# Block 2's stick-breaking: suffix sums collected on VectorE, one product with the -1 matrix a step

## The reference

```python
z = jnp.einsum('bqhd,bkhd->bhqk', qb, k).astype(jnp.float32) * scale
strict = kpos[None, :] < qpos[:, None]
log_beta = jax.nn.log_sigmoid(z)
log_rem = jnp.where(strict, jax.nn.log_sigmoid(-z), 0.0)
suffix = lax.cumsum(log_rem, axis=3, reverse=True) - log_rem
a = jnp.where(strict, jnp.exp(log_beta + suffix), 0.0).astype(v.dtype)
return jnp.einsum('bhqk,bkhd->bqhd', a, v)
```

## Time and profile before

| | us |
|---|---|
| median of 3 runs | 3445.26 |
| lowest and highest run | 3442.79, 3449.83 |
| span of the profiled execution (first to last instruction) | 3442.4 |
| TensorE busy | 3355.2 |
| VectorE busy | 1669.0 |
| ScalarE busy | 1222.1 |

### The profile page before, as it was taken

One profiled execution on the slowest core, in us unless ns is written; L12 is line 12 of the kernel. 1 busy time (PEld: TensorE's weight loads), 2 busy tenths in 40 slices (PEclk: granted clock), 3 DMA queues, 4 the chain that ended last, 5 costly groups with the idle time before them and its releaser, 6 DMA issues. The chain is left out here.

```text
span 3442.4 us, 42159 instructions
## 1 busy us (share of the span) xinstructions
PE 3355.2 (97%) x15712; PEld 2626.8 (76%) x15716; DVE 1669.0 (48%) x2158; ACT 1222.1 (36%) x1831; POOL 238.6 (7%) x268
## 2 busy tenths in 40 slices
PE   8999999999999999999999999999999999999998
PEld 6667888775688877888775688887888776678887
DVE  6755443666444344443636554435443544654433
ACT  4343122432522233332444443324233344543233
POOL 1200000011000000000103300002000101300000
PEclk9999999999999999999999999999999989999999
DMA  6213322221243232332220133333332321023332
GB/s 169 63 48 86 97 98 97 86 80 49 73 103 95 98 104 73 97 98 98 75 64 25 38 103 97 97 98 94 96 94 97 86 74 32 20 86 98 97 98 67
DMA packets 434263, 288.19 MB, mean 84 GB/s; under 512 B 44529, under 2 KB 412317, under 8 KB 433897
## 3 DMA queue, kind: packets, MB, share of 16 engines
q1 hardware_dynamic: 431272, 280.02, 28.1%
q0 software_dynamic: 2736, 4.58, 0.9%
q10 hardware_dynamic: 144, 2.10, 0.2%
HBM read 284.53 MB, written 2.13 MB: 83 GB/s over the span
## 5 line engine op out<-in xcount | busy, mean ns | idle before, releaser
L2022 PE MATMUL bank<-hh,whi 128*128 128x512 f32 x2768 | 1093.3, 395 | 16.2 <-DVE hl L1470 7.2
L2023 PE MATMUL bank<-hl,whi 128*128 128x512 f32 x2768 | 1080.1, 390 | 0.0
L2024 PE MATMUL bank<-hh,wlo 128*128 128x512 f32 x2768 | 1079.9, 390 | 0.0
L1404 DVE TENSOR_TENSOR wlo<-raw,whi 128x1024 fp32r<-128x1024 f32 (+2 forms) x534 | 646.4, 1212 | 312.4 <-ACT whi L945 298.0
L945 ACT ACTIVATE whi<-raw 128x1024 fp32r<-128x1024 f32 (+2 forms) x534 | 546.4, 1034 | 258.3 <-PE bank L2024 257.9
L2022 PEld LDWEIGHTS bank<-hh,whi 128*128 128x128 f32 x2768 | 521.4, 188 | 150.3 <-issue 33.0
L2024 PEld LDWEIGHTS bank<-hh,wlo 128*128 128x128 f32 x2768 | 521.1, 188 | 109.4
L2023 PEld LDWEIGHTS bank<-hl,whi 128*128 128x128 f32 x2768 | 521.2, 188 | 108.3 <-issue 2.6
L2022 PE MATMUL bank<-fshi,whi 128*128 128x512 f32 (+1 forms) x1358 | 526.3, 388 | 3.6 <-ACT G L1090 1.6
L2023 PE MATMUL bank<-fslo,whi 128*128 128x512 f32 (+1 forms) x1358 | 522.6, 385 | 0.0
L2024 PE MATMUL bank<-fshi,wlo 128*128 128x512 f32 (+1 forms) x1358 | 522.5, 385 | 0.0
(11 more groups left out here) (257 smaller groups left out, 2565.9 us busy)
## 6 DMA issues: line engine op xcount, KB each, us to landing
raw<-in_ffn_w_gate SPq DMA_DIRECT2D x88, 512.0 KB, 3.8
raw<-in_ffn_w_up SPq DMA_DIRECT2D x88, 512.0 KB, 3.8
raw<-in_ffn_w_down SPq DMA_DIRECT2D x88, 512.0 KB, 3.5
raw<-in_w_in SPq DMA_DIRECT2D x78, 512.0 KB, 3.9
raw<-in_w_up SPq DMA_DIRECT2D x64, 512.0 KB, 4.0
raw<-in_w_down SPq DMA_DIRECT2D x64, 512.0 KB, 3.4
raw<-in_w_out SPq DMA_DIRECT2D x16, 512.0 KB, 4.0
raw<-in_w_in SPq DMA_DIRECT2D x18, 256.0 KB, 3.4
```

The costliest lines, as they stand in the source:

```text
L1404: dve.tensor_tensor(slot3(wlo, s, m), slot3(raw, s, m), slot3(whi, s, m).bitcast(F32), ALU.subtract).then_inc(c.lo_done.sem, 1)
L2022: pe.matmul(o, wh, ah, start=start, stop=False)
L2023: pe.matmul(o, wh, al, start=False, stop=False)
L2024: return pe.matmul(o, wl, ah, start=False, stop=stop)
```

## The change

A new entry ("sb_add", s) is put behind z_dve for the steps with s % 4 = 1 and 2. In it VectorE adds, in place, the tile of the next key block onto the tile of this one (over the queries that both have), when suf(s) has read it. Tile jt + 1 then holds the sum of all later blocks' softplus, and suf(s) takes one product with `minus` and not two or three. suf(s) for s % 4 = 2 and 3 waits for the sum.

```diff
@@ plan_block2
         if s < n_stick:
             stick_steps.append(("z_dve", s))
+        if s and (s - 1) % QT in (1, 2):
+            stick_steps.append(("sb_add", s - 1))
         if s and s % QT == 0:
@@ VectorE
+                    elif s[0] == "sb_add":
+                        p, jt, zb = stick_step(s[1])
+                        dve.wait_ge(c.sb_suf.sem, c.sb_suf.at(l, s[1] + 1))
+                        later = stick_tile(B_SP, jt)[:, :, P:S - P * jt]
+                        dve.tensor_tensor(later, later, stick_tile(B_SP, jt + 1), ALU.add).then_inc(c.sb_add.sem, 1)
@@ TensorE
                         pe.wait_ge(c.sb_sp.sem, c.sb_sp.at(l, s[1] + 1))
+                        if s[1] % QT >= 2:
+                            pe.wait_ge(c.sb_add.sem, c.sb_add.at(l, stick_sums(s[1] - 1)))
                         for head in range(2):
                             ins = pe.matmul(bank[:, zb + head, 0:n], tri, stick_tile(B_SP, jt)[:, head, :], start=False, stop=jt == QT - 1, skip_group_check=True)
-                            for j2 in range(jt + 1, QT):
-                                ins = pe.matmul(bank[:, zb + head, P * (j2 - jt):n], minus, stick_tile(B_SP, j2)[:, head, :], start=False,
-                                                stop=j2 == QT - 1, skip_group_check=True)
+                            if jt < QT - 1:
+                                ins = pe.matmul(bank[:, zb + head, P:n], minus, stick_tile(B_SP, jt + 1)[:, head, :], start=False, stop=True, skip_group_check=True)
                         ins.then_inc(c.sb_suf.sem, 1)
```

More of the change, by code:

```diff
@@ L622, in counts_of @@
             c.sb_suf = signal("sb_suf", 0, n_stick)
+            c.sb_add = signal("sb_add", 0, SB_H)
             c.sb_a = signal("sb_a", 0, n_stick)
@@ L687, in stick_tile, with stick_sums @@
             return g(at + 2 * SB_AT[jt], 2 * n).rearrange("p (e n) -> p e n", e=2)
+        def stick_sums(s):
+            return 2 * (s // QT) + s % QT
         def stick_step(s):
```

## The result

The changed kernel takes 3468.95 us (median of 4 runs, 3467.49 to 3469.83), the kernel before 3444.03 us beside it (4 runs, 3439.09 to 3449.83). The ratio is 1.0075, with a 95% interval of 1.0062 to 1.0087: 25 us slower. A second comparison, of runs of its own, gave 3467.04 and 1.0065 (1.0044 to 1.0086). The forecast was 3456.5, the range 3449.5 to 3464.

What follows compares the result with a forecast made beforehand. TensorE, busy 97% of the span, bounds the kernel. Waits net of removed work 7.0 us, clock 3.4 + 0.8, together 11.2 us slower: 3445.3 + 11.2 = 3456.5 us, range 3449.5 to 3464.

Steps and rivals of the forecast that it cites:

- the moves are worth more than the arithmetic: suf(2) ahead of nq1, suf(6) ahead of gatesf: a layer loses 3.5 us although 3.48 us of work goes.
- The links: Chain waits on TensorE: z(3) 0.6 us, suf(2) 2.25, z(4) 1.05, suf(7) 6.2; both layers lose 7.0 net.
- The removed work: Products dropped from suf(2), suf(3), suf(6), suf(7): 3.48 us less TensorE work a layer, 6.96 in both.
- The clock term: TensorE's clock falls after waits: 2 x 1.7 us behind suf(7), 0.8 us behind suf(2).
- the one loss at z(3) that is in the old time: Low clock behind the second layer's 2.05 us wait ahead of z(3), priced 1.57 us, already in the old time.
- Rival F: The low clock lingers in four places, adding up to 13 us to the 7: +15 to +20, 3463; chance 0.10.
- A: Work counts, order does not; only the sum ahead of suf(7) shows: gain 5.8 us, 3439.5; chance 0.05.
- B: TensorE fills its waits ahead of suf(2) and suf(7) from nq1 and nkw: 3438.3 us; chance 0.02.
- C: Waits partly taken up by idle links behind them, clock mostly holds: +2 to +6.5, some 3450; chance 0.13.
- D: Waits come as worked out, clock holds or falls once: +7 to +9, some 3453; chance 0.17.
- TensorE's busy time: Sign to look for: TensorE's busy time falls by less than 7 us, as the lower clock adds to it.

Runs made afterwards that it cites:

- order_only: The kernel before's arithmetic (all old products, no sums) in the changed kernel's order: 3455.19 us, ratio 1.0032.
- old_order: The changed kernel with every other entry where it stood before, each sum right behind the next step's z_dve: 3447.65 us, ratio 1.0005.
- padded: old_order plus the removed products done again as useless ones: 3445.23 us, ratio 1.0004.
- after_padded: The changed kernel plus the removed products done again into a bank nobody reads: 3469.85 us, ratio 1.0073.
- after_again: The changed kernel itself measured once more, nothing altered: 3467.04 us, ratio 1.0065.
- best_old_sums: The kernel before, all its products in, with suf_exp(1), z_act(7) and z_dve(7) moved up: 3438.18 us, ratio 0.9990.
- best: The change's arithmetic in the old order, with suf_exp(1), z_act(7), z_dve(7) moved up and each sum behind the suf freeing its tile: 3436.48 us, ratio 0.9978.
- filled_last: The changed kernel with 26 useless products in the wait ahead of suf(7) only: 3460.21 us, ratio 1.0045.
- suf6_moved: old_order with suf(6) moved right behind z(7), ahead of gatesf, step 6's sum behind z_dve(7): 3450.97 us, ratio 1.0027.
- filled: The changed kernel with useless products in two waits a layer, 9 ahead of suf(2), 26 ahead of suf(7): 3454.21 us, ratio 1.0031.

## Why the prediction was wrong, point by point

- **That the moves are worth more than the arithmetic: right.** order_only is slow without the sums, old_order is not slow with them. But the sums more than double what the order costs, as they stand in the waits that it opens.
- **The links: right, nearly to the digit.** z(3) waits 0.62 us (0.6 forecast), suf(2) 2.15 (2.25), z(4) 1.00 (1.05), suf(7) 5.83 (6.2). The last is 0.35 us less, as the swap snks itself waited 0.35 for an eviction; the 6.2 counted that as standing still. All thirteen rows of the table lie within 3.1 us of their links once they are set to one clock, eleven within 1.5.
- **The removed work, 6.96 us: right as work.** padded and after_padded put it back and are 6.4 and 5.8 us slower at equal clock than old_order and after_again.
- **The clock term: wrong, and it is the step that failed.** The prediction put 2 x 1.7 us behind suf(7) and 0.8 behind suf(2), 4.2 us, and nothing anywhere else. By the mean clock it is 17 us, by the profiles at most 17.6, four times as much. The price at the two waits was nearly right. suf(7) took 4.54 and 5.51 us where 3.04 were worked out, 1.5 and 2.5 more, 4.0 for the 3.4 forecast. suf(2) took 3.73 us (1723.35 to 1727.08) and 3.47 in the second layer (2801.58 to 2805.05) where 2.15 were worked out, 2.9 more, less the one loss at z(3) that is in the old time; 0.8 were forecast. Together that is some 1.1 us too little. The other 12 us come from low clock that the prediction took to stay as it was. TensorE's busy time at 0.50 from c00 to suf(3) and from c10 to suf(6) grew from 6.8 to 20.2 us in the first layer (6.7 us of time), which had had little of it, and stayed as it was in the second; some 6 us are outside the pairs. This growth does not come with the moved order alone: over both layers this time is 23.9 us in the kernel before, in order_only and in best_old_sums, all with the old products, and 37.3 in the change, 34.1 in old_order, 30.7 in best, all without them. Nor does the wait ahead of suf(7) make it (40.5 in filled_last); with the one ahead of suf(2) filled too it falls to 27.3. So most of the clock's cost came with the lighter suf steps, in interplay with the wait ahead of suf(2), where the prediction counted their 6.96 us as pure gain.
- **Rival F** (the low clock lingers, +15 to +20) named what happened, with a chance of 0.10, and was itself too small, as it priced four places at 3.3 us each and counted nothing for the lighter suf steps or outside the pairs.
- **Rivals A and B** fell. TensorE waited for VectorE while nkw's products stood behind. C and D fell as well: the links came in full, and the clock did not hold.
- **TensorE's busy time** was to fall by less than 7 us; it rose by 12.8.

**What stays open.** Why lighter suf steps lengthen the low clock was not settled. In three pairs of kernels that differ by the products the one with fewer has the lower clock (old_order 0.9904 and before 0.9930, best 0.9914 and best_old_sums 0.9929, after 0.9880 and order_only 0.9915). Only best and best_old_sums have the same waits. Of the profiles without the old products suf6_moved is the exception, with 23.9 us at the low level at the c groups like the kernels that have them; each of these figures is of one profile. Padding brings the mean clock back in one case (padded 0.9924) but hardly in the other (after_padded 0.9890). It may be that the shorter steps merely shift later groups against whatever times the clock. The 6 us outside the pairs were not tried apart either; the low clock at 880 us is in the first profile of the change and not in its second.

## What to carry to other kernels

Where a list of steps is woven with others by position, one more entry moves all of them: compare the order of every engine before counting the arithmetic, and ask of each moved step what used to cover the chain behind it. Put the new step where nothing waits for it (right behind the one that frees its data), and pin the others. On a kernel that fills TensorE, take the clock as a term of its own for every uncovered wait and for what follows it, and read the mean clock of each run before a difference of a few us is given a cause.

## What was not expected of the hardware

- The same program varies by nearly 13 us, in step with its mean granted clock (3440.7 us at 0.994, 3453.3 at 0.990), so a change of 5 us at the links can be invisible: old_order and best differ from their forecasts by just this.
- Idle time of 2.15 us ahead of suf(2) in each layer cost some 5 to 6 us beyond itself by whole runs, nearly what the 5.8 us ahead of suf(7) did (6.8), and 9.6 us in the stretches of the profiles.
- Useless products in a wait made a kernel 13 us faster (filled against after_again), with the granted clock at 0.992 for 0.988.
